# A mixture-of-experts decoder block: last expert's rows split in halves, last scatter index copied before the wait for its data, final norm shared among three engines

## The reference

```python
def rms_norm(x, g):
    y = xf * lax.rsqrt(jnp.mean(xf * xf, axis=-1, keepdims=True) + NORM_EPS)
    return y * g
...
x = x + hybrid_mixer(rms_norm(x, norm_mix_g), w_in, w_out, pos)
x = x + moe_ffn(rms_norm(x, norm_ffn_g), ...)   # top 4 of 32 experts, each: clamped SwiGLU, 1024 -> 2048 -> 1024
return rms_norm(x, norm_final_g)
```

## Time and profile before

| | |
|---|---|
| median of 3 runs | 1445.6 us (1445.2 to 1447.88) |
| the profiled execution | 1446.0 us, span 1444.2 us |
| busy share of the span | PE 96%, PEld 80%, DVE 85%, ACT 71%, POOL 28% |
| mean granted TensorE clock | 0.985 of full |
| moved | 453 MB, 314 GB/s over the span |
| last MATMUL starts | 1429.21 us |

### The profile page before, as it was taken

The page is one execution under the profiler, slowest core; times in us unless marked ns, Lnnn a source line. Parts: engine busy times, 40 slices in busy tenths (PEclk is TensorE's granted clock), DMA queues, the critical chain, the costliest instruction groups (busy, mean ns, idle before and its releaser), DMA issues.

```text
span 1444.2 us, 19518 instructions
## 1 busy us (share of the span) xinstructions
PE 1387.5 (96%) x6520; PEld 1153.0 (80%) x6520; DVE 1232.4 (85%) x927; ACT 1024.2 (71%) x750; POOL 410.3 (28%) x231
## 2 busy tenths in 40 slices
PE   6999999877999999999999999999999999999995
PEld 5877888766888888888888888888888888888874
DVE  5534547367999999999999999999999999999986
ACT  5234334465788888888888888888888888888874
POOL 0000001284633333333333333333333333333311
PEclk9999999978999999999999999999999999999998
DMA  8221224456999999999999999999999999999993
GB/s 300 94 82 59 100 76 136 157 211 223 379 396 383 381 384 380 372 374 382 378 382 387 370 382 379 377 382 383 381 376 386 380 386 385 381 385 380 372 338 124
DMA packets 81017, 453.48 MB, mean 314 GB/s; under 512 B 13887, under 2 KB 13903, under 8 KB 32736
## 3 DMA queue, kind: packets, MB, share of 16 engines
q1 hardware_dynamic: 68968, 432.55, 75.6%
q0 software_dynamic: 10304, 18.26, 4.9%
q10 hardware_dynamic: 1720, 2.34, 0.5%
HBM read 447.63 MB, written 22.59 MB: 326 GB/s over the span
## 4 chain that ended last, share of the span: by engine, by line
PE 86%; DMA 4%; DVE 3%; POOL 2%; ACT 2%; issue 2%; ACTq 0%; SPq 0%; DVEq 0%; POOLq 0%
PE ps L1722 14%; PE ps L1727 14%; PE ps L1723 14%; PE ps L1685 8%; PE ps L1687 8%; PE ps L1693 8%; PE ps L1415 4%; PE ps L1423 4%; PE ps L1416 4%; DMA acc_rows<-y,idx_scatter 2%; PE ps L1663 2%; PE ps L1676 2%; ACT whi L693 1%; POOL slot_table L611 1%; POOL idx_scatter L601 1%
## 5 line engine op out<-in xcount | busy, mean ns | idle before, releaser
L992 DVE TENSOR_TENSOR wlo<-raw,whi 128x2048 fp32r<-128x2048 f32 x274 | 648.7, 2390 | 108.0 <-ACT whi L693 107.7
L693 ACT ACTIVATE whi<-raw 128x2048 fp32r<-128x2048 f32 x274 | 520.8, 1914 | 137.2 <-PE ps L1727 91.6
L1722 PE MATMUL ps<-whi,xT_hi 128*128 128x512 f32 x992 | 390.4, 394 | 8.3 <-ACT ps L854 8.3
L1723 PE MATMUL ps<-whi,xT_lo 128*128 128x512 f32 x992 | 387.1, 390 | 0.0
L1727 PE MATMUL ps<-wlo,xT_hi 128*128 128x512 f32 x992 | 266.4, 390 | 0.0
L1722 PEld LDWEIGHTS ps<-whi,xT_hi 128*128 128x128 f32 x992 | 187.0, 189 | 47.0 <-issue 8.7
L1727 PEld LDWEIGHTS ps<-wlo,xT_hi 128*128 128x128 f32 x992 | 186.8, 188 | 38.9
L1723 PEld LDWEIGHTS ps<-whi,xT_lo 128*128 128x128 f32 x992 | 187.1, 189 | 37.9
L1685 PE MATMUL ps<-whi,actT_hi 128*128 128x512 f32 x496 | 195.9, 395 | 0.0
L1687 PE MATMUL ps<-whi,actT_lo 128*128 128x512 f32 x496 | 193.2, 390 | 0.0
L601 POOL COPY idx_scatter<-tab 128x1 uint32 (+1 forms) x31 | 59.0, 1904 | 321.9 <-ACT y L841 321.9
(11 more groups left out here) (229 smaller groups left out, 1648.8 us busy)
## 6 DMA issues: line engine op xcount, KB each, us to landing
raw<-in_w_gate_up SPq DMA_DIRECT2D x130, 1024.0 KB, 8.7
raw<-in_w_down SPq DMA_DIRECT2D x126, 1024.0 KB, 9.4
raw_a<-in_w_gate_up SPq DMA_DIRECT2D x63, 1024.0 KB, 6.8
raw_b<-in_w_gate_up SPq DMA_DIRECT2D x63, 1024.0 KB, 7.3
raw<-in_w_in SPq DMA_DIRECT2D x14, 1024.0 KB, 5.2
raw<-in_w_out SPq DMA_DIRECT2D x4, 1024.0 KB, 5.1
x<-in_x SPq DMA_DIRECT2D x4, 512.0 KB, 8.0
acc_rows<-x SPq DMA_DIRECT2D x4, 512.0 KB, 4.9
```

Source lines behind the costliest of these rows:

```text
L693: nc.scalar.activation(whi_slot(n), raw_slot(slot_of(n)), ACT.Copy).then_inc(hi_done, 1)
L992: nc.vector.tensor_tensor(wlo_slot(n), raw_slot(slot_of(n)), whi_slot(n).bitcast(F32), ALU.subtract).then_inc(lo_done, 1)
L1722: mm(ps[:, part, :], xT_hi[:, u, :], w_hi_ap, start=False, stop=False, skip_group_check=True)
L1723: mm(ps[:, part, :], xT_lo[:, u, :], w_hi_ap, start=False, stop=False, skip_group_check=True)
```

## The change

1. The index of the last scatter is copied into `idx_scatter` before GpSimd waits for `y`, not behind that wait.
2. A multiply of 16 elements per partition (`mv`, whose values are no longer used) is put before the memset of `bdn`.
3. `y_hi` and `y_lo` of the last expert are written in two halves of 512 columns; TensorE takes `y_hi` of half 0 for three chunks, then half 1, then waits for both halves of `y_lo`.
4. Final norm: GpSimd writes `with_gain = x1 * gain_row` for chunks 0 and 1 as soon as each is added up; ScalarE scales these by the inverse root and SyncE stores them. VectorE does both inverse roots first and then the row operation for chunks 2 and 3 alone.
5. Tiles: `with_gain` and `square_out` are new names in space that is free by then; three squares go to other scratch tiles.

```diff
-            pl.wait_ge(y_s, E)
             pl.wait_ge(moved, 32 * (E - 2) + 48)
             table_index(idx_scatter, E - 2).then_inc(scatter_index, 1)
             pl.wait_ge(scatter_index, E - 1)
+            pl.wait_ge(y_s, E)
             scatter_rows(moved)
             pl.wait_ge(used, U_ALL - U_DN)
+            link(nc.gpsimd.tensor_tensor(mv[:, :, 0], mv[:, :, 1], mv[:, :, 1], ALU.mult))
             nc.gpsimd.memset(bdn[3 * E:P, :].bitcast(F32), 0.0).then_inc(bdn_zero, 1)
...
+            pl.wait_ge(fin_g_in, 16)
+            for c in range(2):
+                pl.wait_ge(f_sum, c + 1)
+                nc.gpsimd.tensor_tensor(with_gain[:, c, :], x1[:, c, :], gain_row[:, :], ALU.mult).then_inc(hn_gain, 1)
...  # ScalarE
-            nc.scalar.activation(y_hi[:, :], ps[:, 4:6, :].rearrange("p b t -> p (b t)"), ACT.Copy,
-                                 scale=tab[:, E - 1, 1:2]).then_inc(yhi_s, 1)
+            for half in range(2):
+                nc.scalar.activation(y_hi[:, half * UW:(half + 1) * UW], ps[:, 4 + half, :], ACT.Copy,
+                                     scale=tab[:, E - 1, 1:2]).then_inc(yhi_s, 1)
...
+            def final_scale(c):
+                act_e.wait_ge(hn_gain, NC + c + 1)
+                act_e.wait_ge(rstd_s, 3)
+                nc.scalar.activation(with_gain[:, c, :], with_gain[:, c, :], ACT.Copy,
+                                     scale=small[:, 3, c:c + 1]).then_inc(hn_s, 1)
...
             final_root(2)
+            final_scale(0)
+            final_scale(1)
...  # VectorE
-            v.wait_ge(yhi_s, 1)
-            nc.vector.scalar_tensor_tensor(out=y_lo[:, :], ...).then_inc(ylo_s, 1)
+            for half in range(2):
+                v.wait_ge(yhi_s, half + 1)
+                nc.vector.scalar_tensor_tensor(out=y_lo[:, piece], ...).then_inc(ylo_s, 1)
...
             final_sum(3)
-            final_rows(0)
+            final_inverse(0)
             final_variance(2)
-            final_rows(2)
+            final_inverse(2)
+            for c in (2, 3):
+                nc.vector.scalar_tensor_tensor(out=x1[:, c, :], in0=x1[:, c, :], scalar=small[:, 3, c:c + 1],
+                                               in1=gain_row[:, :], op0=ALU.mult, op1=ALU.mult).then_inc(f_out, 1)
...  # TensorE
-            pe.wait_ge(yhi_s, 1)
-            for c in range(NC - 1):
-                last_rows(c, hasT, y_hi, False, False)
-            pe.wait_ge(ylo_s, 1)
+            for half in range(2):
+                pe.wait_ge(yhi_s, half + 1)
+                for c in range(NC - 1):
+                    last_half(c, half, hasT, y_hi, False)
+            pe.wait_ge(ylo_s, 2)
...  # SyncE
-            for c in range(NC):
-                sp.wait_ge(f_out, c + 1)
+            for c in range(2):
+                sp.wait_ge(hn_s, NC + c + 1)
+                sp.dma_start(out[0, c * P:(c + 1) * P, :], with_gain[:, c, :]).then_inc(stored, 16)
+            for c in range(2, NC):
+                sp.wait_ge(f_out, c - 1)
                 sp.dma_start(out[0, c * P:(c + 1) * P, :], x1[:, c, :]).then_inc(stored, 16)
```

More of the change, by code:

```diff
@@ L301, in build @@
     y_lo, _ = place(area + 36 * K, "y_lo", [D], F32R)
+    with_gain, _ = place(area + 48 * K, "with_gain", [2, D])
+    square_out, _ = place(area + 12 * K, "square_out", [D])
     ps = nc.alloc_psum_tensor("ps", [P, 8, UW], F32)
@@ L340, in build @@
     ffn_g_in, router_in = sem("ffn_gain_in"), sem("router_in")
-    hn_s, hn_out, hn_gain = sem("hn_ready"), sem("hn_stored"), sem("hn_times_gain")
+    hn_s, hn_out, hn_gain = sem("rows_scaled"), sem("hn_stored"), sem("rows_times_gain")
     r_tr, rT_s, wr_s = sem("residual_transposed"), sem("rT_ready"), sem("router_weights_ready")
@@ L670, in _ @@
                 pl.wait_ge(has_tr, 1)
-                pl.wait_ge(yhi_s, 1)
+                pl.wait_ge(yhi_s, 2)
                 with pl.Fori(0, NOVER) as i:
@@ L963, in final_square @@
                 act_e.wait_ge(f_sum, c + 1)
-                nc.scalar.activation((y, act, lin, sig)[c][:, :], x1[:, c, :], ACT.Square,
+                nc.scalar.activation((y, lin, sig, square_out)[c][:, :], x1[:, c, :], ACT.Square,
                                      accum_out=small[:, 10, c:c + 1]).then_inc(f_sq, 1)
@@ L1327, in _ @@
                                     ALU.subtract).then_inc(bdn_s, 1)
-            v.wait_ge(yhi_s, 1)
-            nc.vector.scalar_tensor_tensor(out=y_lo[:, :], in0=ps[:, 4:6, :].rearrange("p b t -> p (b t)"),
-                                           scalar=tab[:, E - 1, 1:2], in1=y_hi[:, :].bitcast(F32), op0=ALU.mult,
-                                           op1=ALU.subtract).then_inc(ylo_s, 1)
+            for half in range(2):
+                v.wait_ge(yhi_s, half + 1)
+                piece = slice(half * UW, (half + 1) * UW)
+                nc.vector.scalar_tensor_tensor(out=y_lo[:, piece], in0=ps[:, 4 + half, :], scalar=tab[:, E - 1, 1:2],
+                                               in1=y_hi[:, piece].bitcast(F32), op0=ALU.mult,
+                                               op1=ALU.subtract).then_inc(ylo_s, 1)
             v.wait_ge(act_s, E)
@@ L1377, in final_variance, with final_inverse @@
                 v.wait_ge(f_var, c // 2 + 1)
-            def final_rows(c):
+            def final_inverse(c):
                 v.wait_ge(f_root, c // 2 + 1)
                 inverse_root(small[:, 11, c:c + 2], small[:, 12, c:c + 2], small[:, 3, c:c + 2], small[:, 13, c:c + 2])
-                for k in (c, c + 1):
-                    nc.vector.scalar_tensor_tensor(out=x1[:, k, :], in0=x1[:, k, :], scalar=small[:, 3, k:k + 1],
-                                                   in1=gain_row[:, :], op0=ALU.mult, op1=ALU.mult).then_inc(f_out, 1)
+                v.sem_inc(rstd_s, 1)
             v.wait_ge(fin_g_in, 16)
@@ L1840, in _, with last_half @@
                 last_rows(c, gateT, bdn, True, False)
-            pe.wait_ge(yhi_s, 1)
+            def last_half(c, half, stationary, moving, stop):
+                return mm(ps[:, LAST_BANK[c] + half, :], stationary[:, c * P:(c + 1) * P],
+                          moving[:, half * UW:(half + 1) * UW], start=False, stop=stop)
+            for half in range(2):
+                pe.wait_ge(yhi_s, half + 1)
+                for c in range(NC - 1):
+                    last_half(c, half, hasT, y_hi, False)
+            pe.wait_ge(ylo_s, 2)
             for c in range(NC - 1):
-                last_rows(c, hasT, y_hi, False, False)
-            pe.wait_ge(ylo_s, 1)
-            for c in range(NC - 1):
-                last_rows(c, hasT, y_lo, False, True).then_inc(f_ps, 1)
+                last_half(c, 0, hasT, y_lo, True)
+                last_half(c, 1, hasT, y_lo, True).then_inc(f_ps, 1)
             last_rows(NC - 1, gateT, bdn, True, False)
```

## The result

| | before | changed |
|---|---|---|
| median of 12 runs each, taken in turn | 1445.98 us (1444.92 to 1447.92) | 1448.59 us (1445.64 to 1449.62) |
| ratio | | 1.0016, 95% interval 1.0008 to 1.0023 |
| the profiled execution, its span | 1446.0, 1444.2 | 1449.1, 1447.2 |
| mean granted TensorE clock | 0.985 | 0.984 |
| `y_hi` eviction starts | 1424.27 | 1427.56 |

A forecast was written before the change was run, and what follows sets the result against it. TensorE carries 86% of the chain, but the diff touches only what follows; there four stores become the bound, ending the span at 1443.25 instead of 1444.2. So 1445.6 - 1.0 = 1444.6 us, range 1442.7 to 1447.6.

The forecast's parts named there:

- The switch to multiply code: On GpSimd ahead of the new multiply and bdn memset: loading multiply code was taken to cost 6.46 us.
- a cover that turns into a loss of 0.3: At the bdn memset: done at 1424.1, TensorE wants it at 1423.85, so 4 us of cover become a 0.3 loss.
- rival 3: GpSimd's code switch free (1444.3 us, chance 0.06) or long: ten us instead of 6.46, 3.5 later, 1448.1 us, chance 0.07.
- The loop of experts: The full experts' work ahead of the tail: untouched by the diff, so no change of its time was counted.
- The scatter: Last scatter on GpSimd: with the index copied early its issue ends near 1416.4 and residual loads come 2.2 us sooner.
- Rival 2: Scatter's issue shut out by the second weight subtraction: ends at 1418.6, no earlier load, 1446.8 us; chance 0.12.
- The halves: Last expert's y_hi and y_lo: TensorE reaches y_lo 0.2 us sooner, only if the memset isn't late.
- The final rows: Final norm: last store issued 2.4 us sooner, but four stores become the bound, so the span ends 1.0 us sooner.
- rival 1: Final norm: variance 0 starts after GpSimd's multiply 1 and waits till 1433.85; 1446.5 us; chance 0.19.
- Rival 4: Change does more: VectorE isn't stopped at all beside GpSimd and the code switch is hidden; 1443.7 us; chance 0.11.
- The tail as a whole: End of the kernel: the span was to end at 1443.25 instead of 1444.2, 1.0 us sooner.

The follow-up runs named there:

- e2: The changed kernel with the 16-element multiply moved ahead of GpSimd's wait for y: ratio 1.0007 to the kernel before.
- e4: The changed kernel, unaltered, run again beside others on one chip: ratio 1.0023 to the kernel before.
- h1: The changed kernel with the 16-element multiply put behind the bdn memset instead of ahead of it: ratio 1.0001 to the kernel before.
- f2: The changed kernel with one added wait, so GpSimd clears xg only after VectorE's first slot masks: ratio 1.0019 to the kernel before.
- g1: The changed kernel with 12 filler transposes on TensorE before the last expert's wait for act: ratio 1.0021 to the kernel before.
- e1: The kernel before with only the 16-element multiply added ahead of the bdn memset: ratio 1.0045 to the kernel before.
- g3: The changed kernel without the 16-element multiply ahead of the bdn memset: ratio 0.9996 to the kernel before.
- f1: The kernel before with one added wait, so GpSimd clears xg only after VectorE's first slot masks: ratio 0.9997 to the kernel before.
- g2: The kernel before with only the last expert's y_hi and y_lo in halves: ratio 1.0005 to the kernel before.
- h3: The kernel before with only the last expert's y_hi and y_lo in halves, a second time on another chip: ratio 0.9998 to the kernel before.
- e3: The kernel before with only the scatter index copied ahead of GpSimd's wait for y: ratio 1.0001 to the kernel before.
- h4: As h2, but with the last expert's y_hi and y_lo undivided: ratio 0.9988 to the kernel before.
- h2: The changed kernel without the small multiply, GpSimd and ScalarE taking chunk 0 alone, the xg memset behind the masks: ratio 0.9995 to the kernel before.
- f4: As f3, but GpSimd and ScalarE take chunk 0 alone and VectorE does chunk 1's rows after the first inverse root: ratio 0.9991 to the kernel before.
- f3: The changed kernel with the small multiply ahead of the wait for y and the xg memset behind the first masks: ratio 0.9993 to the kernel before.

## Why the prediction was wrong

- **The switch to multiply code: the step that failed.** The prediction put 6.46 us, the nearest row, and a cover that turns into a loss of 0.3. The place of the memset behind it costs 2 to 3 us by the ratios (e2 and e4, h1 and the changed kernel). In the place it was asked for it took 8.36, 8.70, 8.45, 9.00 and 9.00 (changed, e4, f2, g1, e1). The row was one of the switch to broadcast code; the forecast's own other bound, 25.20 us, was too far to say more than "somewhere below". Its rival 3 named this mechanism, with 3.5 us for a switch of 10 us and a chance of 0.07: at 9.00 that rule gives 2.5 us over the forecast, 1447.1, and in g1 `bdn` did start 2.8 late. The Trainium skill ("GPSIMD Engine Reference", Instruction dispatch) has about 6 us for the first call of freshly loaded code. Here 7.85 to 10.66 were measured in ten kernels, and the measurement decides.
- **What stands behind that wait was left out.** The prediction charged TensorE's wait for the cleared rows at its length. In g1 and e1 the granted clock fell behind the wait, 1.7 us more in g1. This term had no row in the prediction; with it the rule gives 1448.8 for an execution like g1's, beside a measured median of 1448.59. The prediction's last sentence had named both signs of a miss beyond its range, a switch of over 9 us and a loop that changes its time; the first was just reached.
- **The loop of experts at nothing.** `y_hi` came 3.3 us later in the changed kernel's profile. 0.7 of it is the mask collision, 1.6 the fall near 1408; the other 1.0 is unexplained (the start of the last stage differs by 1.7 us among the twelve profiles without the collision). In this one execution the loop and the fall make up most of the miss: the span ended at 1447.2 instead of 1443.25, and of these 4.0 us 3.3 lie ahead of the eviction and 0.7 in the tail. That the switch is the step that failed rests on e1, e2, g3 and h1, not on this profile. The fall isn't the change's alone (f1, g2 and h3 have it too) and in medians the terms can't be added up, since behind a fall the memset is less late.
- **The scatter: right in its place, sized from one execution.** The index was copied at 1393.12 (forecast 1391 to 1394) and the loads followed 6.8 us behind the end of the `y` eviction instead of 10.2. In e3, without a fall, the scatter's issue ended 4.67 us behind the start of the `y` eviction (1416.79 - 1412.12), and the forecast had 1416.4 - 1411.73 = 4.67. Rival 2 fell: loads came sooner in every kernel with the early index. But in g2, h3 and f1 they followed 6.9 to 7.1 us behind `y` without it. So the gain of 1.0 exists only in executions in which the old copy meets the subtractions, and e3's ratio can't tell it from none. In the changed kernel nobody waits for these loads: the additions ran without a break.
- **The halves: right.** 0.16 us (3.43 to 3.27), where 0.2 had been said; 0.17 between h4 and h2.
- **The final rows: right.** Variance 0 took 0.21 us and slipped in ahead of the second multiply (rival 1, 0.19, fell); r times r was stopped for 0.94 us ("over 1"); variance 2 came 6.84 us behind the first addition (6.9), the first store 1.47 behind it (1.65). First store to end of span was 1447.2 - 1440.31 = 6.89 us, by the sum 1.4 + 5.16 + 0.36 = 6.92: the stores bind. What this part brings is small, though: 18.65 with halves alone, 18.48 with the rest (g3). Rival 4 had VectorE not stopped and the switch hidden; f4 shows the first half of that, by giving GpSimd less.
- **The tail as a whole.** Where the switch is hidden (g3) it is 1.45 us shorter than that of before, more than the 1.0 forecast, but only 0.36 shorter than f1's 18.84, where the old copy isn't blocked. Where it isn't, 0.0 to 0.3 shorter, or 3 longer (g1).

**What isn't settled.** Why the lower clock comes so much more often in kernels with the late memset (33 of 50 runs of changed, e1, e4, f2 and g1 against 21 of 126 of before): the wait in the tail is one place for it, the fall near 1408 another. It doesn't follow the length of the idle time before it (a fall behind 1.87 us in f2, none behind 2.60 in g3) nor its end (a fall at 1404.33 in g2, none at 1406.19 in h1). Whether the collision reaches the end in full isn't settled either.

## What to carry to other kernels

- A "warming" instruction isn't free cover: GpSimd works in order, so whatever stands behind the code fetch is late by all of it. Put work that others wait for ahead of it (h1: 2 to 3 us), and look first whether the consumer's own wait hides the fetch; here it did (11.5 us of idle time in g3).
- Count from what an engine's chain really starts at. The `bdn` products came 13.4 to 15.1 us behind the start of the `y` eviction by GpSimd's chain and could have come at 12.35 by TensorE's own, so a gain on TensorE alone brought nothing (g1).
- One profiled execution gives the price of a blocked copy in that execution; before counting on its removal, ask whether it is blocked in the others.

## What the runs showed of the hardware

- The fetch of GpSimd's multiply code took 7.85 to 10.66 us of idle time, the fetch of broadcast code near 288 us 6.2 to 6.7. Of the former 9.01, 8.99, 9.50 and 10.66 are those in which it ran beside the weight loads of the loop.
- A GpSimd memset that starts 0.46 to 0.62 us behind the first of four small tensor_scalar operations of VectorE holds one of them up to the memset's end (1.05 us in six profiles); at 0.81 us or more it doesn't (0.44 in g2, 0.47 in f3). The masks were 0.7 us longer, and the gather as much later.
- A scatter's issue takes 1.58 us where it starts between two of VectorE's weight subtractions, and 2.68 to 2.88 where it starts during one; it then ends 1.5 to 1.7 us behind that one's end (1418.60 against 1417.13 in the kernel before).
- Behind a wait of 2.59 us TensorE's granted clock was 0.52 (1.2 GHz is 0.50), and six products took 2.43 us instead of 1.52 (g1). A fall doesn't come behind every such wait: none behind 2.60 us in g3.
